# Seven half-size products for four more projection pairs of a two-layer encoder trunk, with the left-over ones placed between the heads

## What is computed

```python
def even_mixer(xn, w_in, q_gain, k_gain, rel_bias, w_out):
    u = xn @ w_in
    q, k, v, ub = jnp.split(u, [NA_WIDTH, 2 * NA_WIDTH, 3 * NA_WIDTH], axis=-1)
    ...
def odd_mixer(xn, w_in, gate_bias, h_gain, w_out):
    u = xn @ w_in
    q, k, v, o, gates = jnp.split(
        u, [ML_QK_WIDTH, 2 * ML_QK_WIDTH, 2 * ML_QK_WIDTH + ML_WIDTH, 2 * ML_QK_WIDTH + 2 * ML_WIDTH], axis=-1)
    ...
    h = h * jax.nn.sigmoid(o.astype(jnp.float32))
    return h.astype(xn.dtype) @ w_out
```

## Time and profile before

| | us |
|---|---|
| median of 3 runs | 1143.19 |
| lowest, highest | 1143.02, 1144.21 |
| the profiled execution's own time | 1143.04 |
| its span, first to last instruction | 1140.5 |
| TensorE busy in the span | 854.6 (75%) |
| VectorE, ScalarE, GpSimd busy | 247.7, 169.0, 42.7 |
| share of the 16 DMA engines taken by SyncE's loads | 91.3% |
| read from memory | 436.91 MB |

### The profile page before, as it was taken

How to read it: one execution, slowest core, us unless ns; L and a number is a source line. 1 busy time by engine, 2 the same in 40 slices (tenths; PEclk the granted TensorE clock), 3 DMA queues, 4 the chain that set the end, 5 groups by cost and what they waited for, 6 DMA issues and landing times.

```text
span 1140.5 us, 20331 instructions
## 1 busy us (share of the span) xinstructions
PE 854.6 (75%) x9145; PEld 510.7 (45%) x9145; DVE 247.7 (22%) x790; ACT 169.0 (15%) x459; POOL 42.7 (4%) x48
## 2 busy tenths in 40 slices
PE   9999996656675757666899999966666675666666
PEld 4454663424343434333674556634343442434343
DVE  3651521111011111111234435211110021111111
ACT  2141210101011100001224232111010110101011
POOL 1561000000000000000000000000000000000000
PEclk9999998878889887878999999999787797888788
DMA  9994999999999999999992368999999999999997
GB/s 340 331 347 180 384 425 428 427 427 427 427 426 427 426 428 426 427 427 427 394 335 94 128 266 366 429 427 426 428 427 427 428 425 428 426 427 428 427 425 290
DMA packets 46869, 439.26 MB, mean 385 GB/s; under 512 B 4736, under 2 KB 5984, under 8 KB 21952
## 3 DMA queue, kind: packets, MB, share of 16 engines
q1 hardware_dynamic: 44240, 433.96, 91.3%
q0 software_dynamic: 1088, 2.97, 1.2%
q10 hardware_dynamic: 1456, 1.04, 0.3%
HBM read 436.91 MB, written 1.05 MB: 384 GB/s over the span
## 4 chain that ended last, share of the span: by engine, by line
DMA 54%; PE 39%; DVE 3%; SPq 1%; ACT 1%; issue 1%; POOL 0%; DVEq 0%; ACTq 0%
DMA mem<-in_moe_w_up 45%; PE psum L1446 34%; DMA mem<-in_moe_w_down 7%; PE psum L1610 2%; DMA mem<-in_ev_w_in 2%; PE psum L1722 1%; PE psum L1602 1%; PE psum L1625 1%; SPq L499 1%; PE psum L1463 0%; DVE mem L1054 0%; ACT mem L710 0%; DVE mem L1246 0%; DVE mem L1242 0%; PE psum L1805 0%
## 5 line engine op out<-in xcount | busy, mean ns | idle before, releaser
L1446 PE MATMUL psum<-mem 128*32 128x256 f32 (+6 forms) x7112 | 638.3, 432 | 262.8 <-DMA mem<-in_moe_w_up 224.5
L1446 PEld LDWEIGHTS psum<-mem 128*32 128x32 f32 (+2 forms) x7112 | 345.8, 132 | 525.5 <-issue 423.9
L1102 DVE TENSOR_TENSOR mem<-psum,mem 128x128 f32<-128x128 f32 x62 | 18.1, 291 | 639.6 <-ACT mem L724 622.5
L724 ACT ACTIVATE mem<-psum 128x128 f32<-128x128 f32 x62 | 17.2, 277 | 509.1 <-PE psum L1446 509.1
L1610 PE MATMUL psum<-mem 32*128 32x256 f32 x1024 | 73.4, 401 | 2.9 <-ACT mem L730 2.0
L1446 PE MATMUL psum<-mem,x 128*128 128x128 f32 (+1 forms) x512 | 64.0, 286 | 7.2 <-DVE mem L1054 3.7
L1446 PEld LDWEIGHTS psum<-mem,x 128*128 128x128 f32 x512 | 62.3, 203 | 8.8 <-DVE mem L1054 4.5
L1610 PEld LDWEIGHTS psum<-mem 32*128 32x128 f32 x1024 | 46.4, 184 | 30.6 <-issue 23.4
L1062 DVE TENSOR_SCALAR mem<-cst,mem 128x128 f32<-128x128 f32 x124 | 37.2, 342 | 20.7 <-PE psum L1602 20.7
L730 ACT COPY mem<-psum 128x256 f32<-128x256 f32 x62 | 23.1, 372 | 101.9 <-PE psum L1446 101.9
L726 ACT COPY mem<-psum 128x256 f32<-128x256 f32 x62 | 23.1, 372 | 66.4 <-PE psum L1602 66.3
(11 more groups left out here) (198 smaller groups left out, 329.2 us busy)
## 6 DMA issues: line engine op xcount, KB each, us to landing
mem<-in_moe_w_gate SPq DMA_DIRECT2D x64, 2048.0 KB, 47.3
mem<-in_moe_w_up SPq DMA_DIRECT2D x64, 2048.0 KB, 48.4
mem<-in_moe_w_down SPq DMA_DIRECT2D x60, 2048.0 KB, 43.2
mem<-in_od_w_in SPq DMA_DIRECT2D x6, 2048.0 KB, 21.8
mem<-in_ev_w_in SPq DMA_DIRECT2D x3, 2048.0 KB, 19.0
...
```

The costliest lines, as they stand in the source:

```text
L1102: link(V.tensor_tensor(M["h"], src, M["sg"], ALU.mult))
L1446: return nc.tensor.matmul(out_, lhsT, rhs, start=start, stop=stop)
```

## The change

Three more pairs of blocks are made by seven products each: query and key of phase A, the two gate blocks of phase C, the two value blocks of phase C. 32 matmuls of a pair become 28.

Phase A: the first two products (tile 0 with each half of the query weights) need no sum and stand where tile 0's eight matmuls stood; five more follow, with two weight sums over the key weights and two over the query weights, in place. The activation sums are made before the inverse root of the mean square, in two parts (`x_sums`, `other_sums`). GpSimd's copy of x no longer waits for both tiles. The value products' weight sums get the last three sums for query and key put between them (`last_qk_sums`). SyncE's loads n = 0 and 1 wait for all seven products.

Phase C: VectorE makes four activation sums (`XC`) and two weight sums before it copies the keys, later one more for the gate and one for the values; GpSimd makes four weight sums, 128x2048 each. The gate's raw blocks are summed in `og` and get their sigmoid later, from SBUF. Of the fourteen products, ten stand before the first head and four among the first four heads. The order of the first three expert slots of phase D is changed, and the loads wait for other products.

The diff, cut to what the steps use:

```diff
-                    sp.wait_ge(used["A"], n + 1)
+                    sp.wait_ge(s_qp, 7)
...
                 if n == 0:
-                    sp.wait_ge(used["C"], 4)
+                    sp.wait_ge(s_dl, HEADS)
+                    sp.wait_ge(s_pp, 16)
                 elif n == 1:
-                    sp.wait_ge(s_dl, HEADS)
+                    sp.wait_ge(s_pp, 17)
                 elif n < 4:
...
-            pool.wait_ge(s_load["x"], 16)
-            pool.wait_ge(s_load["x_low"], 16)
             for t in range(TT):
+                pool.wait_ge(s_load["x_low" if t else "x"], 16)
...
+            pool.wait_ge(s_pp, 10)
+            pool.wait_ge(s_ts, 7)
+            pool.tensor_tensor(w_g1[:, lo], w_g1[:, hi], w_g1[:, lo], ALU.subtract).then_inc(s_cg, 1)
+            pool.wait_ge(*arrived["C", 5])
+            pool.wait_ge(s_pp, 11)
+            pool.tensor_tensor(TC3, w_v1[:, hi], w_v1[:, lo], ALU.subtract).then_inc(s_cg, 1)
+            pool.wait_ge(*arrived["C", 4])
+            pool.wait_ge(s_cg, 2)
+            pool.tensor_tensor(w_v1[:, lo], TC3, w_v0[:, lo], ALU.add).then_inc(s_cg, 1)
+            pool.wait_ge(s_pp, 15)
+            pool.wait_ge(s_ts, 8)
+            pool.tensor_tensor(w_v1[:, lo], w_v1[:, hi], w_v1[:, lo], ALU.subtract).then_inc(s_cg, 1)
...
+            act.wait_ge(s_qp, 1)
+            nc.scalar.activation(u_block(0, 1), bank(4), ACT.Copy, scale=inv_rms(0)).then_inc(s_qr, 1)
+            nc.scalar.activation(u_block(1, 0), bank(4), ACT.Copy, scale=inv_rms(1)).then_inc(s_qr, 1)
+            act.dma_start(A["lcst"], a["c_layer0"]).then_inc(s_load["lc0"], 16)
+            act.wait_ge(s_qd, 7)
+            nc.scalar.activation(A["sq"].rearrange("p (t n) -> p t n", t=TT), qk_a, ACT.Square).then_inc(s_qsq, 1)
...
+            act.wait_ge(s_pp, 8)
+            nc.scalar.activation(og[:, 0, 512:1024], bank(0), ACT.Copy, scale=inv_rms(0)).then_inc(s_r1, 1)
+            nc.scalar.activation(og[:, 1, 0:512], bank(0), ACT.Copy, scale=inv_rms(1)).then_inc(s_r1, 1)
...
+            act.wait_ge(s_pp, 13)
+            act.wait_ge(s_r2, 1)
+            p1 = bank(0).rearrange("p (h e) -> p h e", h=4)
+            nc.scalar.activation(ve[:, 0, 4:8, 0:ML_DV], p1, ACT.Copy, scale=inv_square(0)).then_inc(s_r1, 1)
+            nc.scalar.activation(ve[:, 1, 0:4, 0:ML_DV], p1, ACT.Copy, scale=inv_square(1)).then_inc(s_r1, 1)
...
+            def sigmoid(k, n):
+                act.wait_ge(s_cd, n)
+                part = og[:, :, k * 512:(k + 1) * 512]
+                nc.scalar.activation(part, part, ACT.Sigmoid).then_inc(s_og, 1)
+            sigmoid(0, 5)
...
+            def x_sums():
...
+                dve.wait_ge(s_xTv, DC + 2)
+                V.tensor_tensor(XS[2], x1[0], x1[1], ALU.subtract).then_inc(s_xs, 1)
+                V.tensor_tensor(XS[3], x2[0], x2[1], ALU.subtract).then_inc(s_xs, 1)
+                dve.wait_ge(s_xs, 2)
+                V.tensor_tensor(XS[3], XS[3], XS[2], ALU.add).then_inc(s_xs, 1)
...
+            def other_sums():
...
+                dve.wait_ge(*arrived["A", 1])
+                V.tensor_tensor(TQ3, w_k[:, hi], w_k[:, lo], ALU.subtract).then_inc(s_qt, 1)
+                V.tensor_tensor(XS[0], x1[1], x2[1], ALU.add).then_inc(s_xs, 1)
+                dve.wait_ge(s_xs, 4)
+                V.tensor_tensor(XS[1], XS[0], x1[0], ALU.subtract).then_inc(s_xs, 1)
...
             norm(0)
...
+            def qk_sum(to, b_, t, add, n):
...
+                dve.wait_ge(s_qp, n)
+                V.scalar_tensor_tensor(to, bank(b_), inv_rms(t), add, ALU.mult, ALU.add).then_inc(s_qd, 1)
...
+            dve.wait_ge(s_qt, 1)
+            dve.wait_ge(s_qp, 1)
+            V.tensor_tensor(w_k[:, lo], TQ3, w_q[:, lo], ALU.add).then_inc(s_qt, 1)
+            dve.wait_ge(s_qr, 2)
+            qk_sum(u_block(0, 0), 5, 0, u_block(0, 1), 2)
+            qk_sum(u_block(0, 1), 6, 0, u_block(0, 1), 3)
+            qk_sum(u_block(1, 1), 7, 1, u_block(1, 0), 4)
+            dve.wait_ge(s_qt, 2)
+            V.tensor_tensor(w_q[:, hi], w_q[:, hi], w_k[:, lo], ALU.subtract).then_inc(s_qt, 1)
+            qk_sum(u_block(1, 0), 3, 1, u_block(1, 0), 5)
+            V.tensor_tensor(w_q[:, lo], w_k[:, hi], w_k[:, lo], ALU.subtract).then_inc(s_qt, 1)
...
                 V.tensor_tensor(TS["T1"], w_v[:, lo], w_u[:, lo], ALU.subtract).then_inc(s_ts, 1)
+                between()
...
+                        qk_sum(u_block(1, 0), 7, 1, u_block(1, 0), 6)
+                        qk_sum(u_block(0, 1), 3, 0, u_block(0, 1), 7)
+                        qk_sum(u_block(1, 1), 3, 1, u_block(1, 1), 7)
+                    weight_sums(last_qk_sums)
                 if b == 1:
...
+            def og_sum(t, k, b_, add, n):
+                dve.wait_ge(s_pp, 7 + n)
+                V.scalar_tensor_tensor(og[:, t, k * 512:(k + 1) * 512], bank(b_), inv_rms(t), add,
+                                       ALU.mult, ALU.add).then_inc(s_cd, 1)
...
+            def v_sum(t, k, b_, add, n):
+                dve.wait_ge(s_pp, 7 + n)
+                V.scalar_tensor_tensor(ve[:, t, 4 * k:4 * k + 4, 0:ML_DV], bank(b_).rearrange("p (h e) -> p h e", h=4),
+                                       inv_square(t), ve[:, add[0], 4 * add[1]:4 * add[1] + 4, 0:ML_DV],
+                                       ALU.mult, ALU.add).then_inc(s_cd, 1)
...
+            V.tensor_tensor(XC[3], xc_hi[0], XC[1], ALU.subtract).then_inc(s_cx, 1)
+            V.tensor_tensor(XC[2], xc_lo[0], xc_lo[1], ALU.subtract).then_inc(s_cx, 1)
+            dve.wait_ge(*arrived["C", 3])
+            V.tensor_tensor(TC3, w_g1[:, hi], w_g1[:, lo], ALU.subtract).then_inc(s_ts, 1)
+            dve.wait_ge(s_ts, 5)
+            dve.wait_ge(*arrived["C", 2])
+            V.tensor_tensor(w_g1[:, lo], TC3, w_g0[:, lo], ALU.add).then_inc(s_ts, 1)
             copy_u(1)
...
+            og_sum(0, 0, 1, og[:, 0, 512:1024], 2)
+            dve.wait_ge(s_ts, 6)
+            V.tensor_tensor(w_g0[:, hi], w_g0[:, hi], w_g1[:, lo], ALU.subtract).then_inc(s_ts, 1)
+            og_sum(1, 0, 0, og[:, 1, 0:512], 3)
+            og_sum(0, 1, 0, og[:, 0, 512:1024], 3)
             dve.wait_ge(s_aTp, 1)
             V.tensor_copy(C["aT"], mbank(6)[:, 0:64]).then_inc(s_aT, 1)
...
-            for h in range(HEADS):
+            dve.wait_ge(s_cd, 2)
+            og_sum(1, 1, 3, og[:, 1, 0:512], 4)
+            for h in range(4):
+                decay(h)
+            og_sum(1, 0, 3, og[:, 1, 0:512], 5)
+            for h in range(4, HEADS):
                 decay(h)
...
-            copy_u(4)
-            for h in range(4):
-                weigh(h)
+            dve.wait_ge(s_r1, 6)
+            v_sum(0, 0, 1, (0, 1), 7)
+            dve.wait_ge(s_cg, 3)
+            V.tensor_tensor(w_v0[:, hi], w_v0[:, hi], w_v1[:, lo], ALU.subtract).then_inc(s_ts, 1)
+            v_sum(1, 0, 2, (1, 0), 8)
+            v_sum(0, 1, 2, (0, 1), 8)
+            weigh(0)
+            dve.wait_ge(s_cd, 7)
+            v_sum(1, 1, 3, (1, 0), 9)
+            weigh(1)
+            weigh(2)
+            weigh(3)
+            v_sum(1, 0, 3, (1, 0), 10)
+            og_sum(1, 1, 2, og[:, 1, 512:1024], 11)
...
+            product(6, XS[3], w_k[:, hi], True).then_inc(s_qp, 1)
+            pe.wait_ge(s_gc, 1)
+            pe.wait_ge(s_qt, 1)
+            product(7, XS[2], TQ3, True).then_inc(s_qp, 1)
+            pe.wait_ge(s_xs, 5)
+            pe.wait_ge(s_qt, 2)
+            product(3, XS[1], w_k[:, lo], True).then_inc(s_qp, 1)
+            pe.wait_ge(s_qt, 3)
+            pe.wait_ge(s_qd, 3)
+            product(7, x_hi[1], w_q[:, hi], False).then_inc(s_qp, 1)
+            pe.wait_ge(s_qt, 4)
+            pe.wait_ge(s_qd, 4)
+            product(3, XS[0], w_q[:, lo], False).then_inc(s_qp, 1)
             pe.wait_ge(*arrived["A", 3])
...
+            product(0, xc_lo[0], w_g0[:, lo], True).then_inc(s_pp, 1)
+            product(1, xc_hi[0], w_g0[:, hi], True).then_inc(s_pp, 1)
+            pe.wait_ge(s_cx, 4)
+            pe.wait_ge(s_r1, 4)
+            pe.wait_ge(s_ts, 6)
+            product(0, XC[1], w_g1[:, lo], True).then_inc(s_pp, 1)
...
+            product(3, XC[2], TC3, True).then_inc(s_pp, 1)
...
+            pe.wait_ge(s_ts, 7)
+            pe.wait_ge(s_cd, 4)
+            product(3, xc_hi[1], w_g0[:, hi], False).then_inc(s_pp, 1)
+            pe.wait_ge(*arrived["C", 4])
+            product(0, xc_lo[0], w_v0[:, lo], True).then_inc(s_pp, 1)
+            pe.wait_ge(s_dl, 4)
+            m_on_all(1)
+            product(1, xc_hi[0], w_v0[:, hi], True).then_inc(s_pp, 1)
+            pe.wait_ge(s_cg, 3)
+            pe.wait_ge(s_aT, 1)
+            product(2, XC[1], w_v1[:, lo], True).then_inc(s_pp, 1)
+            pe.wait_ge(s_dl, HEADS)
+            ml_scores(0)
+            pe.wait_ge(s_cd, 5)
+            product(3, XC[2], TC3, True).then_inc(s_pp, 1)
+            ml_scores(1)
+            pe.wait_ge(s_ts, 8)
+            pe.wait_ge(s_cd, 9)
```

(12 more changed lines are left out.)

209 lines of the change are left out of this document (88 added, 121 removed).

## The result

The changed kernel takes **1146.58 us** (median of 12 runs), the kernel before, run beside it, 1143.03: a ratio of 1.0023, 95% interval 1.0014 to 1.0032. The forecast was 1137.5, with a range up to 1142.4. Eleven of the 12 runs lie between 1145.6 and 1147.24, and one at 1139.0. The execution that was profiled took 1145.60 us with a span of 1143.4; its counterpart before took 1143.04 with 1140.5.

A forecast was written before the change was run, and what follows sets the result against it. Bound by the mixers' TensorE chains, which move the expert loads one for one: 1143.0 + 0.8 (phase A) - 6.5 (phase C) = 1137.3, plus 0.15 for the runs' median, 1137.5 us. Range for 8 in 10: 1135.6 to 1142.4.

The forecast's parts named there:

- The step that failed: Phase A: from the sum of squares to the fourth value product stays 4.0 us, so that product moves from 46.6 to 47.4.
- my own 0.8 us: Phase A: the forecast term, the phase comes out 0.8 us later, with bounds of 0.0 and 1.5.
- GpSimd holds VectorE: Rival, phase C: GpSimd's sums hold VectorE's decays and readings, +6.3 us in all, 1149.5 us; chance 0.06.
- the clock fell after it: Rival, phase A: TensorE's clock falls in the new 3.2 us idle stretch, 1138.1 to 1139.8 us; chance 0.10.
- stall at the tenth product: Phase C: TensorE waits 0.3 to 0.5 us for VectorE before the tenth product, taken as 0.4.
- The scale: Whole kernel: the time moves by what the two mixers' chains move, one for one, through the expert loads behind them.
- The DMA idle time: Before expert loads begin to depend on TensorE: DMA not full, share 0.57 at 125 to 130 us, 0.37 at 705 to 710.
- the signs that the prediction named: Wrong if a phase C product waits over 1 us, phase A moves over 2 us, or that idle DMA time is gone.
- My inner range: Whole kernel: the forecast's own range, 1135.8 to 1138.9 us, from phase A's bounds, the stall and run scatter; forecast's chance 0.70.

The follow-up runs named there:

- e1: The changed kernel with GpSimd's sum of bias and mask waiting until both VectorE products of query and key by their norms have ended: 1139.27 us.
- e2: The kernel before with the first mixer's half of the change alone: 1152.54 us.
- e7: The changed kernel with GpSimd's sum of bias and mask written as six smaller sums, no order between the engines added: 1138.85 us.
- e9: The changed kernel with the reciprocals of the norms written to PSUM and read there by VectorE's two products: 1138.91 us.
- e10: The changed kernel with GpSimd's sum of bias and mask waiting for only the first of VectorE's two products by the norms: 1139.26 us.
- e4: e1 with the four small transfers of the gains issued by ScalarE behind its copies of the first product: 1138.11 us.
- e8: e4 with three matmuls, whose results are not used, put before TensorE's wait for the key weights: 1137.98 us.
- e5: The kernel before with VectorE's two products by the norms waiting for the same bias and mask loads as GpSimd's sum: 1154.92 us.
- e3: The kernel before with the second mixer's half of the change alone: 1137.67 us.

## Why the prediction was wrong in phase A and right in phase C

**The step that failed** is in phase A: "From there to TensorE's fourth value product [...] it was 46.6 - 42.6 = 4.0 us; now 47.4", with the fourth value product taken as the gate and all that stands behind it in the old place. I followed each VectorE operation up to the sum of squares and then carried the old distance over. In that distance stand the two products with both operands in SBUF, and the row that should have warned me was in my hands: GpSimd's sum at 50.02. Two things had to go wrong for them to meet. By my own 0.8 us they would have stayed 1.0 us apart; VectorE came 1.7 us later. And the bias's arrival, which set GpSimd's start, was not followed at all; it came 1.6 us earlier. The second product had begun 3.1 us ahead of GpSimd's sum (46.95 against 50.02), the two moves together are 3.3, and so GpSimd was first by 0.2. The term was 0.8 and measured 8.0: 1.9 us from the later products, 6.1 from the idle stretch and the slow transposes behind it.

Why the bias was earlier can be read too. GpSimd issues its transfers when the Fourier weights have landed (in the rows, behind the three durations in ns: first and last issue), before and now:

```profile
L613 POOL DMA_DIRECT2D mem<-in_ev_rel_bias x12: 706/724/878, 30.9 to 38.5; - x12
```

```profile
L628 POOL DMA_DIRECT2D mem<-in_ev_rel_bias x12: 683/683/888, 29.5 to 37.2; - x12
```

In six traces (changed kernel, e1, e2, e7, e9, e10) ScalarE issues the 482 KB of the layer's constants at 24.2 to 24.5 us, and the bias's issues begin at 29.5 to 29.6; in the other six it does so at 21.9 to 22.4, and they begin at 30.6 to 30.9. e4 and e8 are among these six although they have the changed first mixer. At the 383 GB/s of the changed kernel from 24 to 30 us, 482 KB are 1.3 us (an estimate), which is about the difference. So the late issue on ScalarE's queue, behind the four gains, seems to have let the Fourier weights, and with them the bias, come sooner; e4's edit takes it back (29.5 in e1, 30.6 in e4), but no run has it without e1's wait.

**The rival that named the mechanism had the wrong place.** "GpSimd holds VectorE" was priced for phase C alone. The Trainium skill ("SBUF — State Buffer", "SBUF: two separate sides") gives the rule of an exclusive lock where both inputs of VectorE lie in SBUF and GpSimd reads SBUF, held for a whole instruction by whichever engine started first; I used it to clear the decays and did not ask which operations it condemns. e5, e7, e9 and e10 agree with it (8.75 us for both products in e5, 7.16 us for GpSimd's sum in e10). And my sentence that GpSimd's sum left a reading alone (0.75 us at 55.62) fits the reason I gave, one operand in PSUM; e9 bears that out.

**The smaller misses of phase A.** The sum of squares began at 44.32 (forecast 43.4), the fourth value product at 48.28 (forecast 47.4). TensorE idled 2.64 us (forecast about 3), but the clock fell after it, which I had given 0.10; and I had let ScalarE's copies be ready when VectorE wanted them, where four issues of transfers held them until 24.35:

```profile
21.83 1.18 ACTq L771 DMA_DIRECT2D small<-in_ev_q_gain  x2
23.04 1.27 ACTq L771 DMA_DIRECT2D small<-in_ev_k_gain  x2
24.35 0.69 ACT L774 ACTIVATE mem<-psum,small 128x512 f32<-128x512 f32 x1 [8.19 <-PE psum L1826]
```

VectorE's first reading waited 1.52 us for them. What each is worth is told by the distance from TensorE's first product behind the landing of the key weights to VectorE's two products by the norms. It is 29.4 us with both losses (47.49 - 18.12, changed kernel), 29.4 with early copies and the clock down (e4), 28.8 with late copies and the clock up (e1, e7, e9, e10) and 27.7 with neither loss (46.06 - 18.39, e8). So early copies alone give nothing back, the clock alone 0.6 us, both together 1.7. My forecast had 25.0 us from the landing to the sum of squares, e8 has 24.5, the changed kernel 26.2.

**Phase C went as forecast.** GpSimd, VectorE's decays, and the reading and score rows before the tenth product:

```profile
607.65 4.50 POOL L666 TENSOR_TENSOR mem<-mem 128x2048 f32<-128x2048 f32 x1 [45.13 <-PE psum L1826]
...
621.05 6.01 DVE L1460 SCALAR_TENSOR_TENSOR mem<-psum,mem 128x256 f32<-128x256 f32 x16 [1.21 <-PE psum L1556]
...
632.86 0.74 DVE L1374 SCALAR_TENSOR_TENSOR mem<-psum,small,mem 128x512 f32<-128x512 f32 x1
...
633.75 7.12 PE L1826 MATMUL psum<-mem 128*128 128x512 f32 x16
```

GpSimd's four sums took 4.50 to 4.54 us (forecast 4.5); the decays 6.0 (6.1); the reading at 632.86 took 0.74 us inside GpSimd's fourth sum (630.84 to 635.38), so it was not held, and there is no stall at the tenth product, where I had 0.4. From the first product to the head loop the chain took 62.7 us (597.25 to 659.92; 68.8 before), where the forecast's own figures give 62.3. What I left out is visible in the chain:

```profile
620.98 7.06 PE psum L1826 x16
629.11 3.63 PE psum L1826 x8
```

In this chain a group of products that follows other work takes 0.2 us more than 3.43 a product, once for each group; five such groups stand before the first head. Less the stall that did not come, this is enough for the difference of 0.4 us, though I did not isolate it.

**The scale held, to half a microsecond.** A mixer's loss and gain came out in the time: 2.1 us at the load against 2.6 in the two profiled executions, for e2 alone 9.3 against 9.7, for e3 alone 6.15 less against 5.7 less. The DMA idle time was still there (share 0.39 from 707 to 712 us, 0.49 from 133 to 138). By the signs that the prediction named, "phase A moves by more than 2 us" is the one that came true.

**A sum that was off.** My inner range ends at 1138.9; with phase A at 1.5, a stall of 0.9 and half a microsecond of scatter its upper end is 1143.2 + 1.5 - 6.0 + 0.5 = 1139.2. Nothing hangs on it.

**The version to keep** is e3, the second mixer's change alone, at 1137.67 us: 0.53% under the kernel before and some 0.8% under the changed one. It has the lowest median and the least code; e4 and e8 can't be told from it.
